# Asking for an expert's down weights ahead of its successor's gate and up weights

## What is computed

```python
def hier_moe(x, ...):                    # 1032 tokens of 1024 values
    # a group of 8 experts is chosen of 4, then 2 experts in that group
    ...
    def expert_mlp(args):
        xb, e = args
        h = jax.nn.silu(xb @ w_gate[e]) * (xb @ w_up[e])   # 1024 -> 512, twice
        return h @ w_down[e]                               # 512 -> 1024
    ys = lax.map(expert_mlp, ...)
    ...                                  # weighted and added back at the tokens' rows
```

## Time and profile before

| | |
|---|---|
| median of 3 runs | 2217.98 us (2217.72 to 2220.22) |
| profiled execution: its own time | 2221.0 us |
| profiled execution: its span | 2219.2 us |
| PE matmul busy | 2058.5 us, 93% of the span |
| VectorE, ScalarE, GpSimd busy | 32%, 17%, 13% |
| bytes moved by DMA | 527.44 MB, of which the weights' queue 491.52 MB |
| mean granted clock of PE | 0.956 of full |

### The profile page before, as it was taken

One profiled execution on the slowest core, in us unless ns is written; L12 is line 12 of the kernel. 1 busy time (PEld: TensorE's weight loads), 2 busy tenths in 40 slices (PEclk: granted clock), 3 DMA queues, 4 the chain that ended last, 5 costly groups with the idle time before them and its releaser, 6 DMA issues.

```text
span 2219.2 us, 31577 instructions
## 1 busy us (share of the span) xinstructions
PE 2058.5 (93%) x12532; PEld 1233.7 (56%) x12532; DVE 704.0 (32%) x1370; ACT 382.3 (17%) x984; POOL 298.3 (13%) x312
## 2 busy tenths in 40 slices
PE   8999999989999999989599999999999989998990
PEld 5666655566555655545366666555765546544550
DVE  4412166671111111111482123767411111111116
ACT  2001123301211111111110111332011111211110
POOL 1200011111111111111331000110011111110104
PEclk9999999999999999989799999999899999998995
DMA  6610013358999999999434110223689999999964
GB/s 226 182 39 29 19 42 116 133 199 317 366 379 383 402 366 382 375 378 345 170 115 115 38 39 11 90 79 130 262 340 367 381 390 380 376 377 372 380 260 158
DMA packets 75368, 527.44 MB, mean 238 GB/s; under 512 B 14554, under 2 KB 23642, under 8 KB 50290
## 3 DMA queue, kind: packets, MB, share of 16 engines
q1 hardware_dynamic: 62162, 491.52, 57.5%
q0 software_dynamic: 13056, 33.84, 6.2%
HBM read 486.21 MB, written 54.60 MB: 244 GB/s over the span
## 4 chain that ended last, share of the span: by engine, by line
PE 88%; DVE 5%; issue 4%; ACT 1%; DMA 1%; POOL 0%; DVEq 0%; SPq 0%; POOLq 0%
PE ps L570 19%; PE ps L869 18%; PE ps L912 10%; PE ps L710 9%; PE ps L865 5%; PE ps L857 5%; PE ps L551 4%; PE ps L840 3%; PE ps L906 2%; PE ps L919 2%; PE ps L891 2%; PE ps L754 1%; PE ps L800 1%; PE ps L657 1%; PE ps L681 1%
## 5 line engine op out<-in xcount | busy, mean ns | idle before, releaser
L570 PE MATMUL ps<-arena 128*128 128x344 f32 x1440 | 421.1, 453 | 0.0
L871 PE MATMUL ps<-arena 128*64 128x256 f32 x1792 | 418.1, 389 | 0.0
L869 PE MATMUL ps<-arena 128*64 128x256 f32 x1792 | 418.0, 389 | 0.0
L570 PEld LDWEIGHTS ps<-arena 128*128 128x128 f32 x1440 | 272.0, 190 | 142.9 <-issue 3.6
L869 PEld LDWEIGHTS ps<-arena 128*64 128x64 f32 x1792 | 237.0, 135 | 164.7 <-issue 23.6
L912 PE MATMUL ps<-arena 128*64 128x512 f32 x448 | 241.4, 689 | 54.7 <-issue 54.6
L914 PE MATMUL ps<-arena 128*64 128x512 f32 x448 | 241.8, 690 | 0.0
L871 PEld LDWEIGHTS ps<-arena 128*64 128x64 f32 x1792 | 236.4, 134 | 0.0
L1830 POOL DMA_INDIRECT ytok<-arena,gidx x64 | 94.0, 1468 | 986.6 <-ACT arena L1165 374.2
L1606 DVE SCALAR_TENSOR_TENSOR arena<-ps,gates,arena 64x256 f32<-64x256 f32 (+1 forms) x128 | 61.1, 477 | 475.2 <-ACT arena L1142 475.2
L710 PE MATMUL ps<-arena 128*128 128x512 f32 x448 | 195.9, 594 | 4.8 <-ACT arena L1090 4.8
(11 more groups left out here) (243 smaller groups left out, 2079.9 us busy)
## 6 DMA issues: line engine op xcount, KB each, us to landing
arena<-in_w_gate SPq DMA_DIRECT2D x64, 2048.0 KB
arena<-in_w_up SPq DMA_DIRECT2D x64, 2048.0 KB
arena<-in_w_down SPq DMA_DIRECT2D x64, 2048.0 KB
arena<-in_w_in SPq DMA_DIRECT2D x36, 512.0 KB, 3.5
arena<-out_y_all SPq DMA_DIRECT2D x16, 512.0 KB, 3.5
xs<-arena SPq DMA_DIRECT2D x16, 512.0 KB, 2.7
ytok<-arena SPq DMA_DIRECT2D x16, 512.0 KB, 3.6
arena<-ytok SPq DMA_DIRECT2D x16, 512.0 KB, 7.5
```

The source lines that it names most:

```text
L570: last = mm(ps[:, 3 * half + ch, 0:CH], wring[:, slot, k * P:(k + 1) * P], xT[:, k, ch * CH:(ch + 1) * CH], start=(k == 0), stop=(k == KD ...
L869: mm(ps[HALF:P, 2 + q, 0:256], xgT[:, slot, k, 0:HALF], wg_half[slot3][q][:, k], start=(k == 0), stop=(k == KD - 1))
L871: last = mm(ps[0:HALF, 2 + q, 0:256], xgT[:, slot, k, 0:HALF], wu_half[slot3][q][:, k], start=(k == 0), stop=(k == KD - 1))
```

## The change

In SP's loop over the experts the two calls change places. For each n from 3 to 31 the down weights of expert n-1 are now asked for first, and the gate and up weights of expert n after them. Waits, buffers, sizes and every other engine stay as they are; the order of the instructions on PE, VectorE, ScalarE and GpSimd is the same in both kernels.

```diff
                 gate_up_in(2, 2, ranked_expert(2))
                 for n in range(3, NE):
+                    down_in(n - 1, (n - 1) % 2, ranked_expert(n - 1))
                     gate_up_in(n, n % 3, ranked_expert(n))
-                    down_in(n - 1, (n - 1) % 2, ranked_expert(n - 1))
                 down_in(NE - 1, 1, ranked_expert(NE - 1))
```

## The result

The changed kernel takes 2234.84 us in the median of 4 runs (2228.54 to 2239.48), the kernel before 2217.85: a ratio of 1.0076, 95% interval 1.0048 to 1.0104. It is slower by 17 us where + 4.8 us was forecast, and outside the range of 2215 to 2229. Two later sets gave 2233.6 and 2235.01 us, ratios 1.0076 (1.0061 to 1.0090) and 1.0073 (1.0060 to 1.0086). The span of the profiled execution is 2226.7 us, 7.5 over that of before.

What follows compares the result with a forecast made beforehand. The prediction took weight transfers through the full DMA queue as the bound. Later starts of expert 31, + 2.35 and + 2.47 us, made + 4.8 on the median of 2217.98: 2222.8 us, range 2215 to 2229.

Steps and rivals of the forecast that it cites:

- What bounds the kernel: In the full stretches of both expert stages, DMA engines never rest; each expert pair is short of weights by 5.2 us.
- Rival 3: Waits at the down product (line 912) were the cost and go: 2133 us, or smaller gains; chance 0.08.
- The start, + 7.21 us a stage: Before the queue is full: it stays full only from 563.82 instead of 556.61 us, 7.21 us later in each stage.
- the sum: Both expert stages together: + 2.35 and + 2.47 make + 4.8 us, or + 2.4 without the slow clock.
- Rival 1: At the start, lost DMA time is made good and the clock costs nothing: 2215.8 to 2222 us; chance 0.28.
- The end, 7.21 - 2.35 and 7.21 - 2.47: At each stage's end most lost time comes back; expert 31 starts only 2.35 and 2.47 us later.
- The price of the slow clock, 1.69 us: At expert 30: after idling ahead of it, PE runs at a lower clock, adding 1.69 us before expert 31.
- The full stretch at nothing: While the queue is full, the 5.2 us a pair only moves from down to gate and up products, costing nothing.
- Rival 4: In SP's requests: the change does nothing because SP reaches both calls together anyway; chance 0.01.
- Rival 2: Around the full experts, near 800 us, the queue runs dry for 2 to 4 us a stage: 2227 to 2231; chance 0.11.

Runs made afterwards that it cites:

- n >= 8: New order only in turns 8 to 31, old order in 3 to 7, against the kernel before: 2217.59 us, ratio 0.9990.
- n >= 26: New order only in turns 26 to 31, old order in earlier turns, against the kernel before: 2213.70 us, ratio 0.9978.
- n >= 30: New order only in turns 30 and 31, against the kernel before: 2211.64 us, ratio 0.9970; again 2215.13 us, ratio 0.9982.
- n >= 6: New order only in turns 6 to 31, old order in 3 to 5, against the kernel before: 2218.88 us, ratio 1.0007.

## Why the prediction was wrong

- **What bounds the kernel:** right. The share of 1.00 and a rate that stays within some 0.5% under either order show a queue that PE's stages wait for, and the waits moved from the down product to gate and up without getting less. Rival 3, that they would go, is refuted: there are 79.6 us of them now.
- **The start, + 7.21 us a stage:** the mechanism is right, and the size nearly. One exchange at n = 5 delays D30 by 7.5 us in the profile and costs 8.4 us a stage in the runs; the turns 3 to 7 together cost 8.35. Two such terms are 16.7 us where the sum had 14.4. Where the queue stands idle is not quite as told: in the changed kernel it is ahead of 545.7, for G3, U3, G4 and U4 are late too, and hardly at 564. Rival 1 held that the DMA engines' uneven finish would make a part of it good, and 2.8 MB missing by 592 us refute it.
- **The end, 7.21 - 2.35 and 7.21 - 2.47, so 9.6 us won back:** this step failed. The runs have 3.7 to 6.4 us for it. It rested on "U30 has the place of D29 and U31 that of D30, both 7.21 later", so on U30 at 1044.76 "at the latest". It landed by 1049.49, 11.9 us behind D29. That is not because D29 was early: in the second stage PE waited for D29 until 2131.59, and U30 came by 2145.26, 13.7 behind it and 11.6 without the 2.1 us by which the stage began later. Nor did it build up in the last experts. U20 came by 867.32, 12.0 behind D19 (855.34):

```profile
867.32 1.93 PE L857 MATMUL ps<-arena 128*32 128x256 f32 x16 [5.19 <-issue]
```

The kernels with a part of the exchanges tell the parts of the delay. The rows are the end of the wait for U30 with n >= 8 and with n >= 26 (line 861 is 857 of the kernel before), and the table counts from the first product of each stage:

```profile
1043.53 1.79 PE L861 MATMUL ps<-arena 128*32 128x256 f32 x16 [4.11 <-issue]
```

```profile
1039.65 1.57 PE L861 MATMUL ps<-arena 128*32 128x256 f32 x24 [2.75 <-issue]
```

| landed by, us into the stage | first stage | second stage |
|---|---|---|
| D29, kernel before | 538.45 or earlier | 538.70 |
| U30, n >= 26 | 540.50 | 538.18 |
| U30, n >= 8 | 545.02 | 541.87 |
| U30, all turns | 550.14 | 550.27 |

With a start as before and few exchanges U30 does have D29's place, within about 2 us as far as it can be seen. The 18 exchanges of the turns 8 to 25 put it 4.5 and 3.7 us further back, and the turns 3 to 7 another 5.1 and 8.4. These are single executions, and those of the changed kernel alone differ by up to 2.1 us here. So the places in the queue were right, and that only the start would move them was wrong.

- **The price of the slow clock, 1.69 us:** it wasn't paid at this place at all. From 1049.49 to 1067.85 and from 2145.26 to 2163.62 are 18.36 us each, the undisturbed length. So one term was 4.7 us too low and the other 1.7 too high in the first stage, + 5.4 instead of + 2.35. The advice of the Trainium skill (TensorE: Matmul & The Clock Gate, Part 1), not to fit a count of slow matmuls, fits what this trace shows here. It would have helped at this place only: the sum without the price was + 2.4, still further from the measured 17.
- **The full stretch at nothing:** this step failed too, by some 2 to 6 us in all. The turns 8 to 25 alone cost 3.7 by the medians and 2.2 by the ratio, and leaving out 8 to 29 of the changed kernel saves 5.9 or 4.0. I had named this as what would upset the sum, that the same transfers take the same time. In the profiles the rate is lower by 2 GB/s of 380, half a percent, or some 2.3 us in 440 of full queue in each stage. That fits the size, but kernels with the order of before in this very stretch have 377 (n >= 26) and 378 (n >= 30) too, so it isn't shown to be the cause.
- **Rival 4, no effect:** refuted by the requests at 564.10 and 565.25.
- **Rival 2, a second dry spell around the full experts:** its sign is there, and its price is small. D17, G18 and U18 are asked for from 799.98 on, 6.3 us later than before and not some 4, and the share just ahead is 0.84 where I had 8 us in hand. Windows of 4 us just before 800 and of 40 us around it, in the kernel before, the changed one, with n >= 6 and (40 us only) with n >= 8:

```profile
796.00:800.00 4.00, 4.00 (x50) 2.25 (x44) 0.48 (x1) 0.38 (x1) 1.76 (x2) 1.00 1.00 419
...
764.00:804.00 40.00, 40.00 (x232) 25.34 (x232) 5.06 (x10) 3.55 (x8) 5.13 (x4) 1.00 0.98 385
```

```profile
796.00:800.00 4.00, 4.00 (x17) 1.56 (x19) 0.22 (x1) 0.22 (x1) 0.00 (x0) 1.00 0.84 356
...
764.00:804.00 40.00, 40.00 (x210) 26.62 (x210) 4.89 (x10) 4.40 (x10) 4.83 (x4) 1.00 0.97 365
```

```profile
796.00:800.00 4.00, 4.00 (x30) 1.63 (x32) 0.69 (x1) 0.58 (x1) 0.00 (x0) 1.00 0.57 238
...
764.00:804.00 40.00, 40.00 (x212) 26.39 (x212) 5.36 (x10) 4.40 (x10) 5.14 (x4) 1.00 0.92 353
```

```profile
764.00:804.00 40.00, 40.00 (x229) 25.33 (x230) 5.34 (x10) 3.81 (x9) 5.14 (x4) 1.00 0.94 356
```

In the changed kernel the share is lower by 0.01 over 40 us, which is 0.4 us of the DMA engines' time. With n >= 8 and n >= 6, where nothing was lost at the start, it is 1.6 and 2.4 us. So a part of what the middle turns cost there can be this, in the first stage. No experiment exchanged these turns alone, so it isn't shown to be the cause.
- **The sum again, with what the runs measured:** + 16.7 at the start, + 2.2 to + 5.9 in the full stretch, - 3.7 to - 6.4 at the end: 12 to 19 us, against 15 to 17 measured. The sum had + 14.4, 0 and - 9.6. Of the 12 us by which it was off, 2.3 are the start's, and the rest the end's and the stretch's, about equal shares as far as the runs tell.

**What stays open.** Three profiled executions of the changed kernel took 2228.54, 2226.92 and 2228.48 us, each the fastest of its set, whose medians are 2233.6 to 2235.0. With turns 3 to 7, 30 and 31 the profiled span is 2227.2 us, the same as the changed kernel's 2226.7, though the medians are 5.9 us apart. So in these two profiles the cost of the full stretch isn't there, while between n >= 8 and n >= 26 it is. What it is stays open: neither the rate nor the share near 800 was shown to be the cause. That the profiled execution of the kernel before was itself 3 us above its median makes the profiles look closer together still. What adds another 0.5 to 1.5 us a stage to the early turns, beyond the missing bytes, is open too.

## What to carry to other kernels

When a queue of loads is the bound, the time that it stands idle while it fills is paid in full at the other end: the exchange of one turn left 2.8 MB unmoved, 7.4 us of the queue's rate, and cost 8.4 us after 500 us of full queue. It is the gap that costs, not the late request: with n = 6 alone, G6 was asked for 6.8 us late (578.04 for 571.20) while other loads were under way, and that cost 1 us a stage. So ask in the order in which buffers come free until the queue is full. In the order of use it paid to ask only for the last loads, and little (3.7 to 6.4 us of 2218). And a wait that is long in the profile says which load is late, not that asking for it earlier shortens the sum.

## What the runs showed of the hardware that was not expected

- The same shortage of weights shows as 79.6 us of waiting in the new order and 54.6 in the old, with a mean granted clock of 0.962 and 0.956. Behind the waits of 2.11 and 2.20 us ahead of expert 30 nothing was lost to the lower clock, where 1.69 us had been lost behind the wait of 1.20 us at the down product. The length of a wait doesn't tell its price.
- The DMA engines moved 434 GB/s in one window of 4 us and 378 to 380 over the stage. Three executions of the changed kernel had 368, 362 and 366 GB/s in the window from 552 to 592, all with a share of 1.01. So a few GB/s between two profiles say nothing about the order of requests.
- Between the request of a down load and that of the gate load behind it SP took 1.16 us (545.70 to 546.86), with the read of the next expert's number in between. Between gate and up, with no such read, it took 0.43 us in the same profile. No run tells whether this costs time here.
